# In each slot ScalarE does its pieces of the front first, the gelu and the scaled diagonals of the pair last

## The reference, cut to what matters

```python
def _peer_block(xb, wq, sub_keys, u_tab, v_tab):
    ...
    top, sel = lax.top_k(cand, PEER_TOPK)
    idx = jnp.take_along_axis(cidx, sel, axis=-1)
    gate = jax.nn.softmax(top, axis=-1)
    u = u_tab[idx]
    h = jax.nn.gelu(jnp.einsum('td,thkd->thk', xb, u).astype(jnp.float32), approximate=False)
    v = v_tab[idx]
    return jnp.einsum('thk,thkd->td', (gate * h).astype(xb.dtype), v)

def _layer(...):
    ...
    x = x + mixed @ w_out
    xn2 = _rmsnorm(x, norm_ffn_g)
    x = x + _peer(xn2.reshape(B * L, D_MODEL), ...).reshape(B, L, D_MODEL)
    gate = jax.nn.sigmoid(_rmsnorm(x, norm_pl_g) @ w_pl_gate)
    x = x + gate * (p @ w_pl)
```

## Time and profile before

| what | value |
|---|---|
| median of 3 runs | 3407.74 us (3406.80 to 3418.14) |
| the profiled execution | 3413.72 us, of it the span of the profile 3411.9 us |
| PE busy | 2416.8 us (71%) |
| DVE busy | 2234.0 us (65%) |
| POOL busy | 1306.0 us (38%) |
| ACT busy | 955.2 us (28%) |
| moved by DMA | 1270.91 MB, mean 372 GB/s |
| mean granted clock of PE | 0.846 |

### The profile page before, as it was taken

How to read it: one execution, slowest core, us unless ns; L and a number is a source line. 1 busy time by engine, 2 the same in 40 slices (tenths; PEclk the granted TensorE clock), 3 DMA queues, 4 the chain that set the end, 5 groups by cost and what they waited for, 6 DMA issues and landing times.

```text
span 3411.9 us, 53263 instructions
## 1 busy us (share of the span) xinstructions
PE 2416.8 (71%) x20824; PEld 966.4 (28%) x20824; DVE 2234.0 (65%) x5457; ACT 955.2 (28%) x2430; POOL 1306.0 (38%) x1142
## 2 busy tenths in 40 slices
PE   3788788745767777765787776757766876677656
PEld 3444233212323333321342221212221322222112
DVE  0114666648667868865667565878777777777764
ACT  1122122214424434421232121323232332223222
POOL 0000443423333433333554533444444445444441
PEclk8888898977888888886887886878887988788878
DMA  8422999999889999999999999999999999999994
GB/s 305 141 84 74 383 421 417 422 371 404 316 332 417 388 389 419 385 401 362 416 412 409 378 406 416 418 420 412 420 419 415 408 420 420 408 417 420 419 417 200
DMA packets 213299, 1270.91 MB, mean 372 GB/s; under 512 B 26640, under 2 KB 29992, under 8 KB 72240
## 3 DMA queue, kind: packets, MB, share of 16 engines
q0 software_dynamic: 159792, 1133.76, 81.1%
q1 hardware_dynamic: 53256, 133.74, 10.4%
HBM read 1238.68 MB, written 28.92 MB: 372 GB/s over the span
## 4 chain that ended last, share of the span: by engine, by line
DMA 28%; PE 13%; DVE 7%; POOL 3%; issue 2%; ACT 2%; DVEq 1%; SPq 0%; another core or an unknown queue 0%; POOLq 0%; ACTq 0%
DMA ring<-in_uv,idx 27%; PE sc L870 6%; DVE ring L1649 4%; PE sc L903 3%; POOL ring L1818 2%; DMA front<-in_c_band_sp 1%; PE route L844 1%; POOL front L1834 1%; ACT diag L1216 1%; PE sc L872 1%; DVEq L1659 1%; PE work L891 1%; ACT hgelu L1211 0%; PE sc L587 0%; PE sc L863 0%
## 5 line engine op out<-in xcount | busy, mean ns | idle before, releaser
L1818 POOL DMA_INDIRECT ring<-in_uv,idx x1056 | 1228.1, 1163 | 1843.2 <-PE sc L872 1402.2
L870 PE MATMUL sc<-ring,diag 32*32 32x512 f32 x8192 | 1254.0, 733 | 691.9 <-ACT diag L1216 669.5
L1649 DVE CUSTOM_DVE_ANT_0 ring<-ring,xn_cur 128x1024 f32<-128x1024 f32 x1056 | 1278.6, 1222 | 648.9 <-DMA ring<-in_uv,idx 644.6
L872 PE MATMUL sc<-ring,diag 32*32 32x512 f32 x8192 | 1253.5, 733 | 0.0
L870 PEld LDWEIGHTS sc<-ring,diag 32*32 32x32 f32 x8192 | 274.2, 118 | 1485.8 <-ACT diag L1216 1126.6
L1211 ACT ACTIVATE hgelu<-hdot 128x2 f32<-128x2 f32 x528 | 107.4, 203 | 1855.2 <-DVE hdot L1649 1852.6
L1216 ACT ACTIVATE diag<-gate_d,hgelu 128x32 f32<-128x32 f32 x1056 | 281.7, 314 | 21.2
L872 PEld LDWEIGHTS sc<-ring,diag 32*32 32x32 f32 x8192 | 272.9, 118 | 0.0
L463 PE MATMUL sc<-big,front 128*128 128x512 f32 x512 | 238.5, 616 | 4.8 <-DVE front L1309 4.8
L1211 ACT ACT_TABLE_LOAD x124 | 159.1, 1283 | 2.2
L844 PE MATMUL route<-big,xnT 128*128 128x256 f32 x576 | 143.6, 405 | 0.0
(11 more groups left out here) (241 smaller groups left out, 2319.9 us busy)
## 6 DMA issues: line engine op xcount, KB each, us to landing
front<-wqk_scratch SPq DMA_DIRECT2D x28, 1024.0 KB
ring<-in_uv,idx POOLq DMA_INDIRECT x1056
ring<-in_wq_t POOLq DMA_DIRECT2D x16, 512.0 KB, 6.5
big<-in_w_in SPq DMA_DIRECT2D x4, 2048.0 KB, 17.4
wqk_scratch<-ring SPq DMA_DIRECT2D x8, 1024.0 KB, 7.4
big<-wqk_scratch SPq DMA_DIRECT2D x8, 1024.0 KB, 14.5
x<-x_scratch SPq DMA_DIRECT2D x12, 512.0 KB
xn_next<-x_scratch SPq DMA_DIRECT2D x9, 512.0 KB, 12.2
```

What stands on the lines that cost most here:

```text
L870: pe.matmul(sc[own, 0, :], diag[own, r, :], uv_rows[own, r, D:D + W4], start=opens_sum, stop=closes).then_inc(row_added[r], 1)
L872: pe.matmul(sc[other, 1, :], diag[own, r, :], uv_rows[own, r, D + W4:2 * D], start=opens_sum, stop=closes).then_inc(row_added[r], 1)
L1649: dve.tensor_tensor_reduce(uv_rows[:, k % RING, 0:D], uv_rows[:, k % RING, 0:D], xn_cur[:, :], 1.0, 0.0, ALU.mult, ALU.add, hdot[:, n % 2, ...
L1818: pool.indirect_dma_start(uv_rows[:, k % RING, :], None, uv, bass.IndirectOffsetOnAxis(ap=idx[:, n % PH, j:j + 1], axis=0)).then_inc(row_i ...
```

## The change

The call of `weigh` moves from the top of ACT's slot to its bottom. No instruction is added or taken away, and no other engine's stream changes.

```diff
@@ -1242,7 +1242,6 @@
                 t, h = n // PH, n % PH
                 for pair in range(PAIRS):
                     s = n * PAIRS + pair
-                    weigh(n, pair)
                     if pair == 2 and h == 4 and t < NT:
                         norm_root(t + 1)
                     if pair == 1 and h == 5 and t < NT:
@@ -1253,6 +1252,7 @@
                     sample_step(s)
                     for i, (_, n0) in enumerate(GATE_JOBS):
                         gate_step(i, s - n0 * PAIRS)
+                    weigh(n, pair)
```

## The result

The changed kernel takes 3511.96 us (median of 4 runs, 3500.64 to 3522.81), the kernel before 3408.35 (4 runs). The ratio is 1.0297, 95% interval 1.0259 to 1.0336: about 101 us slower. Forecast were 3444 with a range up to 3482. The sign was right, the size was not. The profiled execution took 3510.40 us.

What follows compares the result with a forecast made beforehand. The prediction took DMA row fetches as the bound. Turns and band 12.0, `exps` in tiles 4 to 6 16.8 and tile 7 8.3 sum to 37.1 us, giving 3444 us on the median of the runs; range 3408 to 3482.

Steps and rivals of the forecast that it cites:

- What bounds the kernel: Whole kernel: row fetches bound it; an engine costs time only where it holds a ring place until the DMA queue empties.
- First kind: Gates, norms, page copies of slots 201 to 232, nearly all the second half: pieces wait for nothing of their slot, cost 0.
- time is lost after 1600 us, where I count nothing: Stretch after 1600 us: one of the signs that would prove the prediction wrong; the forecast put no cost there.
- Second kind: Slots with `turn_qk` and the band, 6 tiles each: sums start later, 2.0 us a tile, 12.0 us in all (7 to 15).
- Third kind: The 16 `exps` slots of tiles 4 to 7: gelu 7.2 us late, mostly covered; costs 16.8 us plus 8.3 in tile 7.
- the cover: Full DMA queue in the attention: hides 6.5 to 9.7 us of a delay, middle 8.1, set against the 7.2 us late gelu.
- The drain behind a table load: The 16 `exps` slots: the skill's page implies 1.4 us more each, up to 22 us; forecast followed the trace, counting none.
- faster rival: Slots copying turned weights: PE waits less for L1054 and L1059, half of 44.6 us gone, 3397 us; chance 0.07.
- 4 x 0.7 a tile: Four `exps` slots in each of tiles 4 to 7: each 7.2 us delay exceeds a 6.5 us cover by 0.7 us.
- Little is covered: Attention stages: queue nearly always short, so the 16 `exps` delays count in full, 115 us, giving 3535 us; chance 0.08.

Runs made afterwards that it cites:

- e1: Kernel before, with `weigh` last only in the page slots 201 to 233, first elsewhere: 3436.77 us, ratio 1.0065.
- e4: Changed kernel, with each page copy one slot later, first in ACT's slot: 3486.28 us, ratio 1.0214.
- e11: Changed kernel plus two matmuls whose result is never read, ahead of the sums in the 32 page slots: 3486.96 us, ratio 1.0230.
- e3: Kernel before, with `weigh` last only in slots below 64 and from 235 on: 3410.03 us, ratio 0.9996.
- e12: Kernel before, with only roots, projection copies and the copy of normed tokens ahead of `weigh`: 3413.72 us, ratio 1.0008.
- e6: Kernel before, with only the exponentials (24 heads, tiles 2 to 7) ahead of `weigh`: 3436.39 us, ratio 1.0073.
- e7: Kernel before, with only the copies of turned weights, heads' values and normed tokens ahead of `weigh`: 3404.01 us, ratio 0.9982.
- e13: Changed kernel plus four idle matmuls ahead of the sums in the 16 `exps` slots of tiles 4 to 7: 3495.14 us, ratio 1.0245.
- e9: Kernel before, with exponentials, far scores and copies of weights, values and normed tokens ahead of `weigh`: 3476.40 us, ratio 1.0190.

## Why the prediction was wrong

- **What bounds the kernel** (DMA, and an engine only where it keeps a place of the ring until the queue is empty): right behind the attention, and too simple in it. The losses of the tiles 4 to 7 and of the page slots are stretches in which the DMA share fell, and they were not given back. But in the attention DVE did not wait longer for rows (67.1 to 62.3 us). It waited longer for ACT and PE, 70 us in all. These waits run from engine to engine and do not have to empty the queue first.
- **First kind, "waits for nothing of its own slot", page copies at 0: this is the step that failed outright.** The copy L1132 waits for the turn that PE makes in the same slot. I had put the page slots into the kind by the stretch they stand in, not by looking at what releases the piece. They cost 22 to 26 us (e1, e4, e11; the copies waited 158.9 us for PE where it was 8.7 before). The text itself named "time is lost after 1600 us, where I count nothing" as its refutation. The other members of that kind, gates, norms and the gate's sigmoid, did cost nothing: e3 -1 us, e12 +3 us, and lag 100.7 to 100.2 from slot 272 to the end.
- **Second kind, turns and band, 12.0 us, ends 7 to 15:** 17 us (12 to 23) alone. The step itself was right, its sum somewhat small: around 850 PE waited 1.19 us behind the copy of k and 1.13 behind that of the band, where 1.2 and 1.3 were worked out. PE of after, answering to the earlier trace rows:

```profile
854.03 1.06 PE L870 MATMUL sc<-ring,diag 32*32 32x512 f32 x1 [1.19 <-ACT diag L1216]
...
868.53 0.61 PE L870 MATMUL sc<-ring,diag 32*32 32x512 f32 x1 [1.13 <-ACT diag L1216]
```

- **Third kind, `exps`, 16.8 + 8.3 = 25.1 us:** alone it measured 25 (19 to 31). That the two agree is in part luck. In the trace of e6 the tiles 2 and 3, which the sum put at 0, cost some 5 us, and the tiles 4 to 7 cost 3.5, 9.8, 2.8 and 2.6 where 5.6, 5.6, 5.6 and 8.3 stood. The sum also takes the cover once as 6.5 and once as 8.1 us and counts the slot with `route` twice. The rows for the cover are from 2205 and 2265 us; in the attention itself the DMA share was 0.91 in tile 4 and 0.97 to 0.98 in the others before the change, not the 1.01 that the forecast read from 80 us of tile 6. The drain behind a table load that the Trainium skill has (ScalarE: Activation LUTs, "What ACT_TABLE_LOAD costs") would by its figure have added an estimated 22 us and is in no row of after either: the exponentials end at 1029.73, the load begins at 1029.75, and the gelu at 1031.04.
- **What the list of kinds left out: the slots with `far_scores` and with `keep_weights`.** This is the second step that failed. They had no term; `keep_weights` had a part in the faster rival. They stand in the two slots beside each `exps` and wait for PE's work of their own slot (83.5 and 73.1 us). The term "4 x 0.7 a tile" set each late `exps` slot against a cover of its own, as if the slots between them made the delay good. With pieces ahead in all three slots of a head they don't: each late diagonal delays PE's and DVE's work for the next piece. This, not the size of a single delay, turned the 27 us of the single pieces into 65. By tile, 7.6 us were forecast for each of 4 to 6 and 10.3 for tile 7; measured were 9.0, 21.9, 12.7 and 23.4.
- **The faster rival:** its mechanism exists. PE's waits for L1054 and L1059 fell from 44.6 to 28.2 us. With the weights alone ahead the gain is 6 us (e7, interval 1 to 11); 22 were guessed. In the whole change it is buried.
- **"Little is covered", 3535 us, chance 0.08:** nearest in size, but not by its mechanism: it has the 16 `exps` delays count in full because the queue is short, and these alone cost 25 us. 26 us came from a place that it doesn't name.
- **The clock of TensorE** had no term at all. In the page slots it decides whether 26 us are lost.

e7 is the fastest of all kernels here, 0.18% below before. That is within what the prediction counts as no change, though its interval ends at 0.9996.

## What to carry to other kernels

When work in an in-order stream is moved ahead of the instruction that frees a buffer, list for every piece what releases it, slot by slot, and put a piece ahead only if its releaser belongs to an earlier slot. The pages show the cheap mend: the same copy one slot later cost nothing (e4). Where late slots stand in a row, price the densest run by its pace (here some 8 us a slot over three slots, against 6.0 in tile 6 before), not each delay against a full queue. And read which wait ends last on each engine: a DMA share that falls does not tell that rows were missing.

## What the runs showed of the hardware that was not expected

- TensorE's granted clock in the page slots depended on this order. It was 0.73 after, 0.77 in e1 and 0.75 in e13, where PE waited for the diagonals in nearly every slot (after: 31 times, 45.0 us in all). It was 0.83 before (25 times, 35.2 us) and 0.80 to 0.88 in the other kernels whose page slots have no copy that waits ahead of the diagonals and no filler. With two idle matmuls a slot it was 1.00 (9 times, 8.0 us). The sums' median was 612 ns before, 1053 after and 587 with the filler. Useless matmuls gave 25 us back in the changed kernel and nothing in the one before. Adding work can so make a PE that stands in a loop with another engine faster, where the loop is the bound. The Trainium skill speaks of it (TensorE: Matmul & The Clock Gate, "A second HAM failure mode: psum-queue depth-cycling"): a PE that sits idle briefly and often between groups of matmuls falls back to the lower level again and again. These rows agree; what they add is that the fall can come from where another engine's copy stands.
- The same trick in the attention lifted the clock from 0.86 to 0.92 in tile 6 and left the length of this stretch as it was (146.0 to 144.7 us); over the tiles 4 to 7 it gave some 10 us back.

What stays open is how the 38 us of surplus divide between DVE's wait for the diagonals at L1658 and its waits for PE. The first grew from 7.3 to 28.8 us in e9; a kernel with more places for gates, which would take it away, wasn't tried. Nor was one with a deeper ring, which would tell how much of the surplus more rows in flight could hide.
